# Experts' spill in 64-slot blocks of two passes, finished rows scaled on GpSimd

## What is computed

```
xt = rms_norm(h)                      # 2048 x 1024
gates = softmax(top2 of the group's experts) * p_group
for each expert e, rows of the tokens that chose it:
    y = (silu(x @ w_gate[e]) * (x @ w_up[e])) @ w_down[e]     # 1024 -> 512 -> 1024
    h[token] += gate * y
out = rms_norm(h) * final_g
```

## Time and profile before

| | us |
|---|---|
| three runs | 2109.08, 2102.77, 2107.91 |
| median | 2107.91 |
| profiled execution, own time | 2109.44 |
| its span, first to last instruction | 2107.5 |
| busy in the span: PE, DVE, ACT, POOL | 1989.9, 1323.2, 1157.9, 833.3 |
| mean granted TensorE clock | 0.978 of full |

### The profile page before, as it was taken

One profiled execution on the slowest core, in us unless ns is written; L12 is line 12 of the kernel. 1 busy time (PEld: TensorE's weight loads), 2 busy tenths in 40 slices (PEclk: granted clock), 3 DMA queues, 4 the chain that ended last, 5 costly groups with the idle time before them and its releaser, 6 DMA issues. The chain is left out here.

```text
span 2107.5 us, 39825 instructions
## 1 busy us (share of the span) xinstructions
PE 1989.9 (94%) x12627; PEld 1696.8 (81%) x12628; DVE 1323.2 (63%) x2411; ACT 1157.9 (55%) x2421; POOL 833.3 (40%) x1024
## 2 busy tenths in 40 slices
PE   7999999979999999989999688999999999999997
PEld 5888888857777787868778577888888888888886
DVE  5333333338888888845565568777776667795763
ACT  4211111128888889853333267666666657674662
POOL 2322222213656644431332344444444434443443
PEclk9999999989999999999999899999999999999999
DMA  7433333365363543224544579988889988997863
GB/s 224 148 117 120 118 120 121 112 182 151 106 171 99 132 107 91 69 70 161 183 137 150 199 269 367 327 283 299 301 287 313 327 266 295 345 373 241 303 209 87
DMA packets 230708, 420.62 MB, mean 200 GB/s; under 512 B 27290, under 2 KB 165146, under 8 KB 206529
## 3 DMA queue, kind: packets, MB, share of 16 engines
q1 hardware_dynamic: 201312, 351.34, 48.8%
q0 software_dynamic: 29296, 68.03, 12.7%
HBM read 344.35 MB, written 110.41 MB: 216 GB/s over the span
## 5 line engine op out<-in xcount | busy, mean ns | idle before, releaser
L742 ACT ACTIVATE prob<-score,nmax 128x512 f32<-128x512 f32 (+3 forms) x464 | 263.8, 578 | 25.8 <-DVE nmax L892 25.4
L60 PE MATMUL proj<-w_in_lo,n1T_hi 128*128 128x512 f32 (+1 forms) x640 | 243.9, 381 | 3.4 <-DVE w_in_lo L245 3.3
L62 PE MATMUL proj<-w_in_hi,n1T_hi 128*128 128x512 f32 (+1 forms) x640 | 238.8, 373 | 0.0
L892 DVE TENSOR_REDUCE nmax<-score 128x2 f32<-128x1024 f32 (+3 forms) x232 | 212.5, 920 | 41.8 <-PE score L940 40.3
L61 PE MATMUL proj<-w_in_hi,n1T_lo 128*128 128x512 f32 (+1 forms) x640 | 238.7, 373 | 0.0
L60 PE MATMUL u_ps<-wu_lo,xT_hi 128*128 128x256 f32 x752 | 216.9, 288 | 0.0
L61 PE MATMUL u_ps<-wu_hi,xT_lo 128*128 128x256 f32 x752 | 213.4, 284 | 0.0
L62 PE MATMUL u_ps<-wu_hi,xT_hi 128*128 128x256 f32 x752 | 213.4, 284 | 0.0
L1879 DVE TENSOR_TENSOR wg_lo<-raw_pieces,wg_hi 128x1024 fp32r<-128x1024 f32 x124 | 148.0, 1221 | 92.3 <-ACT wg_hi L1840 92.3
L807 POOL TENSOR_SCALAR prob<-prob,scale,lam 128x512 f32<-128x512 f32 (+3 forms) x168 | 136.8, 826 | 154.4 <-DVE scale L879 144.8
L264 DVE TENSOR_TENSOR cosx<-proj,rope_sb 128x512 f32<-128x512 f32 (+1 forms) x64 | 37.8, 591 | 213.3 <-PE proj L62 209.5
(11 more groups left out here) (261 smaller groups left out, 5176.8 us busy)
## 6 DMA issues: line engine op xcount, KB each, us to landing
raw_pieces<-in_w_down SPq DMA_DIRECT2D x64, 1024.0 KB, 10.6
raw_pieces<-in_w_gate SPq DMA_DIRECT2D x62, 1024.0 KB, 8.2
raw_pieces<-in_w_up SPq DMA_DIRECT2D x62, 1024.0 KB, 7.7
qk_scratch<-qkT SPq DMA_DIRECT2D x94, 256.0 KB, 2.6
xT_sb<-in_xT SPq DMA_DIRECT2D x16, 512.0 KB, 5.0
h<-in_x SPq DMA_DIRECT2D x16, 512.0 KB, 6.5
acc_scratch<-h SPq DMA_DIRECT2D x16, 512.0 KB, 3.1
n_scratch<-n SPq DMA_DIRECT2D x16, 512.0 KB, 5.6
```

Of the source, the lines that this page charges most:

```text
L60: pe.matmul(out, hi, w_lo, start=first, stop=False)
L62: return pe.matmul(out, hi, w_hi, start=False, stop=last)
L742: act.activation(prob[:, n % RING, c, 0:w], score[:, n % BUFS, c, 0:w], ACT.Exp, bias=nmax[:, c, n:n + 1], accum_out=part[:, c, n:n + 1]). ...
L892: dve.tensor_reduce(nmax[:, :, n:n + 1], score[:, n % BUFS, :, 0:w], AX.X, ALU.max, negate=True).then_inc(max_ready, 1)
```

## The change

1. The first 128 rows of an expert form a full block, which does three passes as before. What goes over 128 is put into blocks of 64 slots, which run ahead of the full block. In a small block the 64 columns of the high part of x and the 64 of its low part stand side by side as one stationary tile of 128 (`xT[:, k, HP:HP + P]`), so two passes (w_lo and w_hi) give both halves, one in partitions 0 to 63 and one in 64 to 127, and lo·w_lo as well. Halves are added by a product with two stacked identities (`fold`, 128x64), which also turns them: eight full-precision matmuls of 64 columns in place of four turns. Ahead of these ScalarE copies g and u out of PSUM. The two halves of y are added by ScalarE (scaled lower half to `y_part`) and VectorE.
2. The slot list has 31 blocks of 64 for an expert in place of 16 of 128 (992 columns instead of 512), and is read in three transfers; `ends` goes, and the router does one more step on each tile.
3. In full blocks the scaling of finished rows moves from VectorE (one instruction) to GpSimd (two); in small blocks it stays on VectorE.
4. GpSimd's order in a block changes: the store and the fetch stand behind the gather, ahead of the add.
5. In full blocks ScalarE's square stands behind silu, and the casts of pieces 1 and 2 ahead of it.
6. Gather and add leave out padding rows by a bounds check (1920 padding rows were moved each way before).

The core of the diff:

```diff
-SLOT_BLOCKS = SEQ // P
+HP = P // 2
+SLOT_BLOCKS = 1 + (SEQ - P) // HP
...
+                def normalize(b, e):
+                    pool.wait_ge(rstd_ready, b + 2)
+                    pool.wait_ge(stored, b * 16 + 16)
+                    pool.sem_inc(passed, 1)
+                    pool.tensor_scalar(whole[:, :], whole[:, :], rstd[:, :], None, ALU.mult).then_inc(whole_scaled, 1)
+                    pool.wait_ge(whole_scaled, e + 1)
+                    pool.tensor_tensor(final[:, :], whole[:, :], g_bc[:, :], ALU.mult).then_inc(final_ready, 1)
+
+                def one_block(b, after):
+                    pool.wait_ge(x_in, b * 16 + 16)
+                    pool.sem_inc(passed, 1)
+                    gather(b + 1, within(after))
+                    store(b, b * 2 + 4)
+                    fetch_whole(b)
+                    add(b)
+                    normal_root(b)
...
+                def full_block(b, e, replaced):
...
+                    normalize(b, e)
+                    aim_store(b)
+                    move_on(b)
+                    pool.tensor_copy(own[:, :].bitcast(I32), slots[:, bass.ds(within(e), 1), :].bitcast(I32))\
+                        .then_inc(own_ready, OWN_STEPS)
...
+                def small_block(b, e, n, left):
+                    act.wait_ge(g_done, b + 1)
+                    act.wait_ge(h_turned, b * 2 + 1)
+                    act.copy(hid[:, :], g_ps[:, :]).then_inc(part_out, 1)
+                    act.wait_ge(y_ready, b + 1)
+                    act.wait_ge(u_done, b * 2 + 1)
+                    act.copy(u_part[:, 0:HALF], u_ps[:, 0, 0:HALF]).then_inc(part_out, 1)
+                    square(b)
+                    act.wait_ge(h_turned, b * 2 + 2)
+                    act.activation(act_g[:, :, :], fold_ps[:, 0:KF, :], ACT.Silu).then_inc(silu_ready, 1)
...
-                    highs(0)
-                    square(b)
-                    highs(1, 2)
+                    highs(0, 1, 2)
                     act.wait_ge(g_done, b + 1)
                     act.wait_ge(h_turned, b * 2 + 1)
                     act.activation(hid[:, :], g_ps[:, :], ACT.Silu).then_inc(silu_ready, 1)
+                    square(b)
                     highs(3, 4, 5)
...
                     lows(0, 1, 2)
-                    normalize(b)
...
+                def packed_product(out, packed, w_hi, w_lo, first, last):
+
+                    pe.matmul(out, packed, w_lo, start=first, stop=False)
+                    return pe.matmul(out, packed, w_hi, start=False, stop=last)
+
+                def fold_parts(out, raw, ks):
+                    for i, k in enumerate(ks):
+                        mm = pe.matmul(out[:, i, :], raw[:, k * P:(k + 1) * P], fold[:, :], start=True, stop=True)
+                    return mm
```

More of the change, by code:

```diff
@@ L1766, in move_on @@
                     pool.sem_inc(passed, 1)
-                def one_block(b, e, replaced, here, after):
+                def normalize(b, e):
[6 more added lines that the diff above has]
+                def one_block(b, after):
                     pool.wait_ge(x_in, b * 16 + 16)
@@ L1771, in one_block @@
                     gather(b + 1, within(after))
+                    store(b, b * 2 + 4)
+                    fetch_whole(b)
                     add(b)
-                    scale(b)
-                    store(b)
+                    normal_root(b)
+                def small_block(b, e, n, left):
+                    one_block(b, (left - 1) * N_EXPERTS + e)
+                    aim_store(b)
                     move_on(b)
-                    pool.tensor_copy(own[:, :].bitcast(I32), slots[:, bass.ds(within(here), 1), :].bitcast(I32))\
+                    pool.tensor_copy(own[:, :].bitcast(I32), slots[:, bass.ds(within(left * N_EXPERTS + e), 1), :].bitcast(I32))\
@@ new lines, in _ @@
+                listed = slots_d.rearrange("(p b) c -> p (b c)", p=P)
+                slot = slots[:, :, :].rearrange("p b c -> p (b c)")
+                SMALL = slice(3 * N_EXPERTS, None)
+                pool.dma_start(slot[:, 0:3 * N_EXPERTS], listed[:, 0:3 * N_EXPERTS]).then_inc(slots_in, 16)
+                for half in range(2):
+                    pool.dma_start(slot[half * HP:(half + 1) * HP, SMALL], listed[HP:, SMALL]).then_inc(slots_in, 16)
+                for padding in (own, pads):
+                    pool.dma_start(padding[:, :], empty_d.rearrange("(p b) c -> p b c", p=P)[:, 0, :]).then_inc(own_free, 16)
@@ L1783, in _ @@
+                pool.memset(x[:, :], 0.0).then_inc(x_cleared, 1)
                 pool.memset(y[:, :], 0.0).then_inc(y_ready, 1)
+                pool.tensor_tensor(fold[:, :], ident[:, 0:HP], ident[:, HP:], ALU.add).then_inc(fold_ready, 1)
+                first_smalls = small_count(pool, 1)
                 pool.wait_ge(own_free, 32)
-                gather(0, 0)
+                pool.wait_ge(slots_in, 48)
+                pool.wait_ge(x_cleared, 1)
+                gather(0, within(first_smalls * N_EXPERTS))
@@ L1808, in _ @@
                 pool.tensor_tensor(last_stat[:, 2:3], last_stat[:, 1:2], power[:, 0:1], ALU.pow).then_inc(last_step, 1)
-                store(blocks)
+                store(blocks + 1, blocks * 2 + 5)
                 pool.wait_ge(last_step, 5)
@@ L1832, in copy_hT, with small_block, full_block @@
                         .then_inc(hT_ready, 1)
-                def one_block(b, e, replaced, here, after):
+                def small_block(b, e, n, left):
+                    act.wait_ge(g_done, b + 1)
[7 more added lines that the diff above has]
+                    act.activation(act_g[:, :, :], fold_ps[:, 0:KF, :], ACT.Silu).then_inc(silu_ready, 1)
+                    act.wait_ge(u_done, b * 2 + 2)
+                    act.copy(u_part[:, HALF:], u_ps[:, 1, 0:HALF]).then_inc(part_out, 1)
+                    copy_xT(b + 1)
+                    act.wait_ge(y_done, b + 1)
+                    act.wait_ge(own_ready, (b + 2) * OWN_STEPS)
+                    act.activation(y_part[HP:P, :], y_ps[0:HP, :, :].rearrange("p a b -> p (a b)"), ACT.Copy,
+                                   scale=own[0:HP, 1:2]).then_inc(y_scaled, 1)
+                def full_block(b, e, replaced):
                     def highs(*ks):
@@ L1904, in hidden, with small_hidden, small_block, full_block @@
                         .then_inc(hid_ready, 1)
-                def one_block(b, e, replaced, here, after):
+                def small_hidden(b, half):
+                    ks = slice(2 * half, 2 * half + 2)
+                    up = fold_ps[:, KF:, :] if half == 0 else late_ps
+                    dve.wait_ge(silu_ready, b + 1)
+                    dve.wait_ge(h_turned, b * 2 + (half + 2))
+                    dve.tensor_tensor(act_h[:, ks, :], act_g[:, ks, :], up, ALU.mult).then_inc(hid_ready, 1)
+                    dve.wait_ge(hid_ready, b * 2 + (half + 1))
+                    dve.tensor_copy(hT[:, ks, 0:HP], act_h[:, ks, :]).then_inc(hT_ready, 1)
+                    dve.wait_ge(hT_ready, b * 2 + (half + 1))
+                    dve.tensor_tensor(hT[:, ks, HP:P], act_h[:, ks, :], hT[:, ks, 0:HP], ALU.subtract).then_inc(hT_split, 1)
+                def small_block(b, e, n, left):
+                    small_hidden(b, 0)
+                    small_hidden(b, 1)
+                    split_xT(b + 1)
+                    normalize(b)
+                    dve.wait_ge(y_done, b + 1)
+                    dve.wait_ge(y_scaled, n + 1)
+                    dve.scalar_tensor_tensor(out=y[HP:P, :], in0=y_ps[HP:P, :, :].rearrange("p a b -> p (a b)"),
+                                             scalar=own[HP:P, 1:2], in1=y_part[HP:P, :],
+                                             op0=ALU.mult, op1=ALU.add).then_inc(y_ready, 1)
+                def full_block(b, e, replaced):
                     def lows(*ks):
```

182 lines of the change are left out of this document (120 added, 62 removed).

## The result

The changed kernel takes 2356.66 us (median of 4 runs, 2354.44 to 2361.28) against 2108.49 for the kernel before (median of 4): 1.1185 times as long, with a 95% interval from 1.1157 to 1.1213. The sign was forecast, the size was not: 248 us are lost where 23 were expected, and the range ended at 2168. The profiled execution took 2361.28 us, with a span of 2359.3.

A forecast was written before the change was run, and what follows sets the result against it. TensorE paces most blocks, with GpSimd's loop about as long; that loop and the shared port take the gain. Singles +18.7, pairs +1.5, start +2.5 make +22.7 on a 2107.5 span, 2130.2; forecast 2131 us, range 2066 to 2168.

The forecast's parts named there:

- What bounds the kernel: Experts' part: TensorE paces most blocks at 18.1 us; GpSimd's loop beside it is about as long, 19.7 a turn.
- The small block: Second block of two-block experts (pairs): 14.4 us on TensorE against 18.14, saving 3.7 a pair.
- The new order: GpSimd's block loop: own copy to add takes 7.7 us instead of 6.4; with 13.3 behind the add, a turn is 21.0.
- The scaling: Full blocks: GpSimd's two products take 1.4 and 1.94 us; collisions cost VectorE 3.3 for the 1.28 it loses.
- they overlap, so I take 20.2: One-block experts (singles): GpSimd's loop and VectorE's shared port give nearly the same length, 20.2 us each, from 18.1 to 21.5.
- the add's flight of 12 hides: GpSimd's queue: argument that 5 us of work ahead of the slot copies hides in the add's flight.
- rival 4: Scaling waits for splits and delays slot copies, lengthening GpSimd's loop by 1.0 a block: 2178 us, half 2155; chance 0.15.
- the 36.3: GpSimd's two turns in a two-block expert (pair), one add flight short: 36.3 us against 36.2 before.
- the 56 us of the prediction: TensorE in the 15 small blocks: 3.7 us saved a pair, 56 in all, stalls apart.
- The start: Loading the slot lists by five transfers instead of two, about twice the bytes: +2.5 us, between 1.8 and 6.
- The padding: Padding rows skipped in gather and add: nothing counted, since flights differ by what else is loading.
- Rival 2: TensorE's saving shows through shorter add flights and half-hidden scaling: 2058 us, half 2083; decides below mean flight about 9; chance 0.35.

The follow-up runs named there:

- experiment 5: The kernel before with only the small blocks, their slot lists and the skipped padding; order, scaling and square stay as before: 2159.95 us, 1.0255 times the kernel before.
- 10 to 12: Experiment 5 with square and scaling in the middle of full blocks; with the small block's y freed of the landed add; with both: 2152.0, 2147.9 and 2148.5 us.
- experiment 8: The kernel before with GpSimd's new order, the square behind silu and VectorE's scaling behind the split of x: 2225.8 us, +118.7.
- experiment 6: The kernel before with the scaling of all blocks by two GpSimd products behind the root, in the old order: 2176.9 us, +69.8.
- experiment 7: The kernel of experiment 6 with VectorE's weight splits cut to a few columns: 2113.4 us.
- Experiments 1 to 3: The changed kernel with GpSimd scaling only 8 of 1024 columns; with scaling back on VectorE; with the fetch directly behind the own copy: 2228.1, 2252.4 and 2237.4 us.
- experiment 1: The changed kernel with GpSimd scaling only 8 of the 1024 columns of finished rows, all waits kept: 2228.1 us.
- experiment 13: Experiment 5 with square and scaling in the middle of full blocks, the small block's y freed of the landed add, and the gather one block further ahead: 2104.65 us, 1.0001.
- experiment 9: The kernel before with only the padding rows left out of gather and add by the bounds check: 2100.36 us, 0.9962 times the kernel before.

## Why the prediction was wrong

- **What bounds the kernel**: right. GpSimd's list is about as long as TensorE's block, and whatever TensorE gains is given back to it (experiments 5, 10 to 12).
- **The small block** at 14.4: right, 13.97 in experiment 5.
- **The new order**: the mechanism was right, the size was low. In the turn of experiment 8 it is 9.15 from own copy to add instead of 7.7, and 22.7 in all instead of 21.0. My 6.4 for the kernel before was one row; its singles average 7.6, and those of experiment 8 10.5. I took mean issue times; in the list they come at 1.94 and 1.97, and the fetch copy waits 1.8 for the counts of the next expert, which in the kernel before lay behind the fetch's issue. And the 7.0 that I read as a pair's short flight ends at the issue of a store, which waits for VectorE's scaling; those adds landed 6.5 after their issue on average.
- **The scaling**: mis-sized, 6.3 instead of 3.3 (experiment 6); 5.25 without the splits beside it (experiment 7). The half-width row from which I took 1.4 gave the product with a scalar at half its price, 2.85, and even twice that row is 1.85. VectorE's loss, in turn, was over-priced: its splits of the gate and up pieces took 37 us longer than before, 1.2 a full block and not 3.3, about what the moved scaling saved it. The direction of the Trainium skill, "GPSIMD Engine Reference", section 4.1, elementwise products on VectorE, agrees with the runs: 1.28 us there, 5.25 here. The estimate of 2.25 for the second product, from the table in section 3.1 of the same page of the Trainium skill, was nearer the measured 2.40 than my 1.94.
- **The step that failed** is "they overlap, so I take 20.2", with "the add's flight of 12 hides" the scaling, which I held against rival 4. I laid root and scaling beside the add's flight and did not ask when they may start. The root needs the square, the square the fetched rows, and the new order issues that fetch only just ahead of the add: it lets the square start 9.05 us later, and the add lands as the scaling begins. So fetch, square, root, 7.2 of scaling, copies, gather and store follow one another, 27.7 in the turn shown; a single takes 28.5 instead of 20.2, and the flight hides nothing of the scaling. Experiments 1 to 3 show it: taking out the scaling, or issuing the fetch earlier, gives about 6 to 6.6 back in each single.
- **In pairs** the same step failed where I left scaling out of the 36.3. GpSimd's two turns average 41.1, as long as the pair: 9.4 and 8.5 from own copy to add, 10.3 behind the first add, and behind the second 12.9, where I had a short flight of 7.6. That stretch holds the fetch's landing, square, root and 5.3 of scaling. But taking the scaling out does not bring the pair back: the 12.9 falls to 7.8, the 10.3 rises to 12.1, and the pair is still 39.9 (experiment 1). What else lengthens it was not taken apart; the small blocks in the old order cost 38.6 already (experiment 5).
- **TensorE's clock** is missing from the sum. Its shorter work in the small blocks should have lowered its busy time by the 56 us of the prediction; it rose by 25, from 853.4 to 878.0, at a granted clock of 0.88. So about 80 us, an estimate, are slower products behind waits; experiment 13, with the same products at 0.99, is busy for 72 us less. How much of this lengthens the blocks is open, since GpSimd's turn by itself is already as long as a single.
- **The start**: 2.5 was 10.9, of which the slot lists are 6.6; the rest differs from run to run.
- **The padding** at nothing: alone it is worth 7 us (experiment 9).
- **The rivals**: rival 4 named the place and the direction but priced it by one collision, 1.0 a block; the loss is 9.5 a single and 4.9 a pair. Rival 2 was to decide once the mean flight is below about 9. My row had the median, 11.7, where the mean was 10.0. In the changed kernel the mean is 8.2 (median 9.5), so the condition was met, and yet the rival failed, for the turn of a full block no longer hangs on the flight.

Open: how much of experiment 6's loss is VectorE's delay and how much GpSimd's turn, and why singles take 19.9 in experiment 13. TensorE has no large wait left there, but GpSimd waits 171.5 us in 47 pieces for the square, and its turn averages 19.6 in singles: fetch, square, root, gather, store and copies are still one chain. That this chain sets the pace is not shown.

## What to carry to other kernels

Before work is put into the shadow of a transfer on an in-order queue, follow what it needs back to the issue of that transfer and walk one whole turn of the queue with it; if its own input comes by a transfer issued in the same place, nothing is hidden. A saving on TensorE shows only as far as the loop beside it has slack, so shorten that loop first: skipping padding alone paid, and the small blocks came level only when the gather was taken out of the list's wait. Price a moved operation by a run on its new engine beside its new neighbours.

## What was not expected of the hardware

A product of GpSimd with a per-partition scalar, in place over 128x1024, took 2.85 us alone, longer than the product of two tensors over the same shape (2.40); beside VectorE's splits the first grew to 3.85 and the second not at all in experiment 6, while the splits of the up pieces went from 1.22 to 1.59; in the singles of the changed kernel the second took 3.4 as well. And a wait of TensorE cost more than its length: behind 6.87 us idle it ran at a granted clock of 0.50 for 4.5 us.
